# Moving GpSimd's two-tensor products to VectorE and ScalarE in a two-layer hybrid decoder step

## What is computed

```python
xn = rmsnorm(x, norm_mix)
zq, zk, zv, hq, hf, hi, hg, u, zg = split(xn @ w_in)
q, k = rope(rmsnorm(zq), pos), rope(rmsnorm(zk), pos)       # x1*cos - x2*sin, ...
p = e / (sum(e) + exp(sink - m))                            # attention weights
o_b = p @ v
qh = silu(hq)                                               # hq * sigmoid(hq)
S_new = exp(G_last) * S + (kc * exp(G_last - G)).T @ ic     # HGRN2 state; an output
o_a = rmsnorm(o, onorm) * silu(hg)
gates = sigmoid(zg)                                         # 3 x 1024 columns
x = x + sum_n(gates[n] * (branch[n] @ w_branch[n])) @ w_o
x = x + square(relu(rmsnorm(x) @ w_up)) @ w_down
```

## Time and profile before

| | |
|---|---|
| median of three runs | 1057.27 us (1057.12 to 1058.95) |
| the profiled execution: time, span | 1057.55 us, 1055.7 us |
| TensorE busy | 1010.8 us (96%), 7342 products |
| VectorE busy | 697.5 us (66%) |
| ScalarE busy | 501.2 us (47%) |
| GpSimd busy | 179.9 us (17%) |
| mean granted TensorE clock | 0.979 |

### The profile page before, as it was taken

The page is one execution under the profiler, slowest core; times in us unless marked ns, Lnnn a source line. Parts: engine busy times, 40 slices in busy tenths (PEclk is TensorE's granted clock), DMA queues, the critical chain, the costliest instruction groups (busy, mean ns, idle before and its releaser), DMA issues.

```text
span 1055.7 us, 18186 instructions
## 1 busy us (share of the span) xinstructions
PE 1010.8 (96%) x7342; PEld 976.8 (93%) x7342; DVE 697.5 (66%) x943; ACT 501.2 (47%) x740; POOL 179.9 (17%) x113
## 2 busy tenths in 40 slices
PE   6999998979999999999999999798899999999998
PEld 6989998969799999999998999798888999999998
DVE  6678776664887555555757787757558865555556
ACT  6428562236255444444554377332552554535354
POOL 0154021225430000000002441305055100000000
PEclk9999998989999999999999999999799999999999
DMA  7554542323365555555564553432334756555552
GB/s 274 178 185 137 183 150 80 101 80 92 121 249 174 164 161 170 162 165 160 170 216 132 175 202 102 132 107 73 100 100 127 271 161 176 162 161 161 173 162 84
DMA packets 43680, 161.87 MB, mean 153 GB/s; under 512 B 5120, under 2 KB 6400, under 8 KB 43040
## 3 DMA queue, kind: packets, MB, share of 16 engines
q1 hardware_dynamic: 42512, 151.73, 45.9%
q0 software_dynamic: 1104, 9.24, 2.2%
HBM read 152.69 MB, written 10.29 MB: 154 GB/s over the span
## 4 chain that ended last, share of the span: by engine, by line
PE 79%; DVE 12%; issue 4%; ACT 3%; POOL 1%; DMA 0%; DVEq 0%; ACTq 0%; POOLq 0%
PE pz L398 70%; PE pm L398 9%; DVE w_lo L949 3%; DVE arena L1149 2%; POOL arena L1438 1%; ACT w_hi L717 1%; DVE arena L1150 1%; DVE arena L1165 1%; DVE arena L1235 1%; PE pm L527 0%; DVE small L1124 0%; ACT a_hi L736 0%; DVE arena L1180 0%; ACT h_hi L926 0%; DVE arena L1199 0%
## 5 line engine op out<-in xcount | busy, mean ns | idle before, releaser
L398 PE MATMUL pz<-a_hi,w_hi 128*128 128x288 f32 x1376 | 418.3, 304 | 11.8 <-DVE w_lo L957 8.3
L949 DVE TENSOR_TENSOR w_lo<-raw,w_hi 128x1024 fp32r<-128x1024 f32 x267 | 351.4, 1318 | 92.8 <-ACT w_hi L717 92.5
L398 PE MATMUL pz<-a_lo,w_hi 128*128 128x288 f32 x1376 | 409.5, 298 | 0.0
L398 PE MATMUL pz<-a_hi,w_lo 128*128 128x288 f32 x1376 | 408.4, 297 | 0.0
L717 ACT ACTIVATE w_hi<-raw 128x1024 fp32r<-128x1024 f32 x267 | 279.5, 1051 | 193.4 <-PE pz L398 189.5
L398 PEld LDWEIGHTS pz<-a_hi,w_hi 128*128 128x128 f32 x1376 | 262.1, 190 | 15.6 <-issue 10.4
L398 PEld LDWEIGHTS pz<-a_lo,w_hi 128*128 128x128 f32 x1376 | 262.5, 191 | 1.2 <-issue 0.8
L398 PEld LDWEIGHTS pz<-a_hi,w_lo 128*128 128x128 f32 x1376 | 262.6, 191 | 0.0
L398 PE MATMUL pz<-h_hi,w_hi 128*128 128x288 f32 x768 | 230.0, 300 | 2.8 <-DVE h_lo L1244 2.8
L398 PE MATMUL pz<-h_lo,w_hi 128*128 128x288 f32 x768 | 227.2, 296 | 0.0
L398 PE MATMUL pz<-h_hi,w_lo 128*128 128x288 f32 x768 | 226.4, 295 | 0.0
(11 more groups left out here) (171 smaller groups left out, 728.9 us busy)
## 6 DMA issues: line engine op xcount, KB each, us to landing
raw<-in_w SPq DMA_DIRECT2D x268, 512.0 KB, 3.6
arena<-in_s SPq DMA_DIRECT2D x2, 2048.0 KB, 9.0
out_ss_out<-arena POOLq DMA_DIRECT2D x2, 2048.0 KB, 9.7
out_u_out<-arena POOLq DMA_DIRECT2D x2, 864.0 KB, 7.4
arena<-in_kcT SPq DMA_DIRECT2D x2, 512.0 KB, 6.0
arena<-in_vc SPq DMA_DIRECT2D x2, 512.0 KB, 7.4
out_kc_out<-in_kc_kept POOLq DMA_DIRECT2D x2, 496.0 KB, 10.2
out_vc_out<-in_vc_kept POOLq DMA_DIRECT2D x2, 496.0 KB, 11.1
```

The source lines that it names most:

```text
L398: return nc.tensor.matmul(out, a, b, start=start, stop=stop, **kw)
L949: tt(w_lo[:, r], raw[:, r], f(w_hi[:, r]), ALU.subtract).then_inc(s["w_lo"], 1)
```

## The change

GpSimd keeps the pooling sums, the memsets, the branch sums and its DMAs. All its other work on two tensors goes elsewhere: the cosine product, the normalising of the attention weights and the two products with sigmoids to VectorE; the masks `im` to ScalarE, as copies scaled by a column of `bmask`; the gate tiles are read by VectorE with the norm's factor, as all other tiles are, and `scale_gates` and `read_gate` are gone. The decay of the state is fused with the sum: VectorE does state x decay + new part for each sample and head (32 instructions per layer). TensorE's products for it and VectorE's updates stand in the first turn of the feed-forward, after units 1, 3, 5 and 7 and in turns 2 to 9; the masks are written in turns 54 to 61.

```diff
@@ tensor: unit, hgrn, ffn_turn
-                    elif U_GATE <= t4 < T_BR:
-                        pe.wait_ge(s["z_read_act"], read_act(l, t4))
                     else:
                         pe.wait_ge(s["z_read_dve"], read_dve(l, t4))
...
-                if 53 <= u <= 56:
-                    h = u - 53
-                    if h < 2:
-                        pe.wait_ge(s["o_rstd"], l + 1)
...
+            def sample_states(l, h):
+
+                if h < 2:
+                    pe.wait_ge(s["rstd"], 2 * l + 2)
+                    pe.wait_ge(s["o_rstd"], l + 1)
+                else:
+                    pe.wait_ge(s["snew_read"], 4 * l + (h - 1) + HEAD)
+                pe.wait_ge(s["imask"], 4 * l + (h + 1))
+                im = (KK, D1, X1, ZF)[h]
+                for half in range(2):
+                    last = mm(PM[2 * (h % 2) + half], ktok_s[0:NS, h], im[0:NS, half * 512:(half + 1) * 512])
+                last.then_inc(s["snew"], 1)
...
                     if first and j == 0:
-                        pe.wait_ge(s["snew_read"], 4 * l + 4 + HEAD)
                         norm_sum(2 * l + 2)
+                    if first and j in (1, 3, 5, 7):
+                        sample_states(l, j // 2)
@@ scalar
-                    act.wait_ge(s["gate_z"], 3 * l + (3 - n))
+                    act.wait_ge(s["z_read_dve"], read_dve(l, U_GATE + (3 - n) * KT - 1))
...
+                if 54 <= u < 62:
+                    h = (u - 54) // 2
+                    im = (KK, D1, X1, ZF)[h]
+                    for b in range(4 * (u % 2), 4 * (u % 2) + 4):
+                        last = act_fn(im[0:NS, b * P:(b + 1) * P], itok[0:NS, 2, h], ACT.Copy,
+                                      scale=c("bmask", slice(0, NS))[:, b:b + 1])
+                    if u % 2:
+                        last.then_inc(s["imask"], 1)
...
-                    if U_GATE <= u < U_BR:
-                        read_gate(l, u)
@@ vector
+                elif t >= U_GATE:
+                    out = gate_tile(t)
...
+                    tt(qk_rs.rearrange("p (j t) -> p j t", t=T), qk.rearrange("p (j t) -> p j t", t=T), bc(cos, 5),
+                       ALU.mult).then_inc(s["qk_cos"], 1)
...
+                for g in {18: (0, 1, 2, 3), 20: (4, 5, 6)}.get(u, ()):
+                    hs, o = (GRP, g * 4) if g < 2 else (2, 8 + 2 * (g - 2))
+                    v = p_samp if g == 6 else prob[:, g].rearrange("p (a n) -> p a n", a=hs)
+                    for a in range(hs):
+                        last = ts_(v[:, a], v[:, a], rec[:, o + a:o + a + 1], None, ALU.mult)
+                    last.then_inc(s["prob_n"], 1)
...
+                    tt(ZQ, ZQ, D0, ALU.mult).then_inc(s["hz_q"], 1)
...
+                if u == 30:
+                    dve.wait_ge(s["sig"], 3 * l + 3)
+                    tt(ZG, ZG, D1, ALU.mult).then_inc(s["silu_g"], 1)
...
-                    tt(S0v[:, :, h], S0v[:, :, h],
-                       pm[:, b0:b0 + 2].rearrange("p c (b n) -> p (c b) n", n=P), ALU.add).then_inc(s["snew_read"], 1)
+            def sample_states(l, j):
+
+                h, half = (j - 2) // 2, j % 2
+                if half == 0:
                     dve.wait_ge(s["snew"], 4 * l + (h + 1))
...
+                for b in range(4 * half, 4 * half + 4):
+                    z = PM[2 * (h % 2) + half][:, (b % 4) * P:(b % 4 + 1) * P]
+                    last = stt(S0v[:, b, h], S0v[:, b, h], es[:, b * H + h:b * H + h + 1], z, ALU.mult, ALU.add)
+                if half:
+                    last.then_inc(s["snew_read"], 1)
...
+                    if first and 2 <= j < 10:
+                        sample_states(l, j)
                     if j + LEAD < 16 or not last:
                         split(l, U_FFN + j + LEAD, i)
...
-                    if u < U_GATE:
+                    if u < U_BR:
                         read_tile(l, u)
...
-                with dve.Fori(0, FI - 1) as i:
-                    mlp(l, i, False, True)
+                mlp(l, 0, False, True)
+                with dve.Fori(0, FI - 2) as i:
+                    mlp(l, i + 1, False)
                 mlp(l, FI - 1, True)
```

More of the change, by code:

```diff
@@ L72 @@
 T_BR, T_O, T_FFN = 50, 74, 82
-ACT_READS = T_BR - U_GATE
-DVE_READS = U_GATE + (T_FFN - T_BR) + 16 * FI
+READS = T_FFN + 16 * FI
 C = {}
@@ L307, in read_dve @@
         def read_dve(l, t):
-            return l * DVE_READS + (t + 1 if t < U_GATE else t + 1 - (T_BR - U_GATE)) + HEAD
-        def read_act(l, t):
-            return l * ACT_READS + (t + 1 - U_GATE)
+            return l * READS + (t + 1) + HEAD
         def first_norm(j):
@@ L389, in _ @@
             for j0, j1 in pieces:
-                sp.wait_ge(s["z_read_dve"], DEPTH * DVE_READS + HEAD - (KT - j1))
+                sp.wait_ge(s["z_read_dve"], DEPTH * READS + HEAD - (KT - j1))
                 sp.dma_start(io["y"][:, j0:j1], x[:, j0:j1]).then_inc(s["y_out"], 16)
@@ L432, in unit @@
                     if t4 < 0:
-                        pe.wait_ge(s["z_read_dve"], l * DVE_READS + HEAD)
-                    elif U_GATE <= t4 < T_BR:
-                        pe.wait_ge(s["z_read_act"], read_act(l, t4))
+                        pe.wait_ge(s["z_read_dve"], l * READS + HEAD)
                     else:
@@ L745, in norm @@
                 act_fn(rstd[:], rstd[:], ACT.Exp, scale=-0.5).then_inc(s["rstd"], 1)
-            def read_gate(l, t):
-                act.wait_ge(s["unit_done"], l * UNITS + (t + 1) + HEAD)
-                act_fn(gate_tile(t), PZ[t % 4][:, 0:T], ACT.Copy).then_inc(s["z_read_act"], 1)
             def attention(l, u):
@@ L1051, in attention @@
                     nc.vector.reciprocal(rec, den).then_inc(s["rec"], 1)
+                    dve.wait_ge(s["rec"], l + 1)
+                for g in {18: (0, 1, 2, 3), 20: (4, 5, 6)}.get(u, ()):
[4 more added lines that the diff above has]
+                    last.then_inc(s["prob_n"], 1)
                 if u == 25:
@@ L1113, in hgrn @@
                 if u == 27:
+                    dve.wait_ge(s["sig"], 3 * l + 1)
+                    tt(ZQ, ZQ, D0, ALU.mult).then_inc(s["hz_q"], 1)
                     dve.wait_ge(s["sig"], 3 * l + 2)
@@ L1184, in hgrn @@
                     tt(a_lo[:, 0:4], hv(X0), f(a_hi[:, 0:4]), ALU.subtract).then_inc(s["oa_lo"], 1)
-                if 54 <= u <= 57:
-                    h = u - 54
+            def sample_states(l, j):
+                h, half = (j - 2) // 2, j % 2
+                if half == 0:
                     dve.wait_ge(s["snew"], 4 * l + (h + 1))
-                    dve.wait_ge(s["s0_decay"], l + 1)
-                    b0 = 2 * (h % 2)
-                    tt(S0v[:, :, h], S0v[:, :, h],
-                       pm[:, b0:b0 + 2].rearrange("p c (b n) -> p (c b) n", n=P), ALU.add).then_inc(s["snew_read"], 1)
+                for b in range(4 * half, 4 * half + 4):
[3 more added lines that the diff above has]
+                    last.then_inc(s["snew_read"], 1)
             def keep_diagonal(l):
@@ L1361, in _ @@
                 q5 = qk.rearrange("p (j t) -> p j t", t=T)
-                tt(qk_rs.rearrange("p (j t) -> p j t", t=T), q5, bc(cos, 5), ALU.mult).then_inc(s["qk_cos"], 1)
                 nc.gpsimd.memset(uext[:, :, 0:PAD], 0.0).then_inc(s["u_front"], 1)
@@ L1395, in _ @@
                 tt(pool_d[:, :, 0:PAD], first, uext[:, :, PAD:2 * PAD], ALU.subtract).then_inc(s["pool_first"], 2)
[L1397 to L1414, removed]
                 pool.wait_ge(s["sfin"], l + 1)
@@ L1421, in _ @@
                 pool.dma_start(io["sp_out"][l].rearrange("p h n -> p (h n)"), ZI[:, 0:512]).then_inc(s["sp_out"], 16)
[L1422 to L1431, removed]
                 for d in range(KT):
```

## The result

The changed kernel took 1025.09 us, the median of four runs (1025.03 to 1026.71), beside 1057.19 for the kernel before on the same chip: a ratio of 0.9685, with a 95% interval from 0.9667 to 0.9703. The forecast was 1027.0 with a range of 1014 to 1039. The profiled execution took 1025.03 us (span 1023.2), 32.5 under that of before; the mean granted clock rose from 0.979 to 0.995, GpSimd's busy time fell from 179.9 to 69.7 us, and VectorE's too, from 697.5 to 678.9, with more work on it.

What follows compares the result with a forecast made beforehand. TensorE was taken as the bound nearly everywhere, with stops caused by GpSimd holding VectorE. Removed 41.1 less 5.0, 3.5, 0.9 and 1.2 gives 30.5 us; 1057.5 - 30.5 = 1027 us, range 1014 to 1039.

Steps and rivals of the forecast that it cites:

- The cause: TensorE's stops at HGRN levels 0 and 5: GpSimd's products hold VectorE's instructions, though no wait names GpSimd.
- The removed 41.1 us: Both layers: split waits before unit 31 (2.6 us), four line 1166 waits (24.0) and slow clock behind them (14.5) go.
- Level 0, 2 x 2.5 us: HGRN level 0, each layer: VectorE's gate reading waits for unit 33's end, so TensorE waits 2.5 us; 5.0 given back.
- Its slow clock, 3.5 us as the half of 7.0: After level 0's wait, both layers: half the old slow-clock loss (4.0 + 3.0) stays, 3.5 us; ends 0 and 7.0.
- Levels 5 and 6 and the last keep, 0.9 us: Ahead of unit 48, one unit barely covers VectorE's chain: 0.15 us at each of three places, 0.9 us in all.
- The transposes, 1.2 us: Behind unit 20: normalising on VectorE delays the pooled branch's low halves, a new 0.6 us wait per layer, 1.2 us.
- The wait at the branches' end stays at 1.4: Branches' end, line 1244: TensorE's wait of 1.4 us stays as it is in the sum.
- Free by cover: Query, gate and cosine products, feed-forward state updates and ScalarE's masks fit in idle or covered time and cost nothing.
- level 0 comes free: Rival: level 0's wait falls under some 1.3 us, nothing slow follows: 1021 us; chance 0.18.
- The tied ring: Rival: VectorE's turn, ScalarE's split and the next turn form a ring stopping TensorE at all seven levels: 1079; chance 0.06.

Runs made afterwards that it cites:

- the small products: Cosine product, normalising of the probabilities and the two sigmoid products put back on GpSimd, against the changed kernel: 1034.23 us.
- the late reading: VectorE reads unit 33's gate tile behind that turn's state work and level 0 instead of ahead, against the changed kernel: 1017.78 us (0.9620).

## Why the prediction was right

**The cause** (GpSimd holds VectorE): right, and shown by putting the decay and the gate products back one at a time. The masks alone were not put back. The parts add up only roughly. By the medians they are +18.0 us for the decay and +9.1 for the small products (on different chips) and +6.4 for the gates (on one chip), 33.5 against 32.1 for all; by the profiled executions +17.8, +6.0 and +5.1, 28.9 against 32.5. Slow running that falls otherwise makes much of the difference: in the profiled execution of the small products level 0 of layer 1 has 0.3 us of it in place of 1.8, and the start of layer 2 none in place of 1.5.

**The removed 41.1 us**: right. All four stops on the level product of before went; level 0's became another, smaller one.

**Level 0, 2 x 2.5 us**: measured 2 x 2.2, at the place and by the mechanism named, as the late reading shows. **Its slow clock, 3.5 us as the half of 7.0**: 1.8 + 1.8 = 3.6. This was luck: with the same wait other executions had 0.3 or 3.4 us in layer 1 (the last section), and no row said a half.

**Levels 5 and 6 and the last keep, 0.9 us**: the list of waits has 0.5, all of it at the last keep (L1237), but the distance has 1.4. From level 5's products to the products of unit 50 it is 28.35 us (209.10 to 237.45), before 30.92 with 3.3 of slow running in it: 0.7 us a layer more. With the gate products back on GpSimd it is 27.62 again, so VectorE's gate readings cost it, as forecast; the size was too small.

**The transposes, 1.2 us**: the step that failed. Their first eight start at 95.86, before at 95.91, and take 1.09 in place of 0.87. From the units ahead (74.60, before 74.71) to the unit behind (96.96, before 96.78) it is 0.3 us more, in layer 2 as well: 0.6 in place of 1.2. VectorE's low halves did come 1.5 us later (95.30 against 93.75); the mistake was that two of four had to be done. In the program the first four transposes need one. The length of the normalising was forecast as 2.8 and came to 2.71, but for a wrong reason. By shape, on VectorE:

```profile
L1057 DVE TENSOR_SCALAR arena<-arena,small 128x256 f32<-128x256 f32 x16 | 4.5, 349 | 0.0
...
L1057 DVE TENSOR_SCALAR arena<-arena,small 128x128 f32<-128x128 f32 x16 | 3.3, 281 | 0.1
```

128 more columns cost 68 ns, 0.53 ns a column. The Trainium skill (VectorE: DVE Perf Modes, the perf-mode tier table) gives such products two a cycle, which at that page's 0.96 GHz is 0.52 ns: the trace agrees, and I had rejected it. The 358 ns for 288 columns of the earlier trace rows was one point, and by this rate some 205 ns of it are fixed time; a rate takes two.

**The wait at the branches' end stays at 1.4**: 1.57. But the slow stretch behind it in layer 1 went (28.38 us for 198 products before, 26.66 after), which the sum did not have: 1.7 us. It gave back 1.5 at the start of layer 2, where 24 products take 4.91 us in place of 3.39 behind a wait of VectorE's that was there before.

**Free by cover**: right for the updates, to 0.01 us. Four masks took 1.26 us and not 1.0; moving them away gained nothing. The sum had the move of the state into the feed-forward at nothing. Against standing in the mix with the same work on VectorE it brought 3.6 us; but before, VectorE had only four sums a layer there, so this is a cost avoided and no part of the 32.5.

In sum it is 32.5 us measured against 30.5. By the distances between the same points of the two chains, the changed kernel gained more than the forecast at the waits of levels 0 and 5 (0.9), at the transposes (0.6), and from the products of unit 50 to the start of layer 2 and to the end (2.1 and 0.6, of which 1.7 is the slow stretch that went). It gained less at levels 5 and 6 and the last keep (0.5), in the slow clock of level 0 (0.2) and at the starts of the layers (1.6, of which 1.5 is that of layer 2). Together this is 1.9 us.

The rival "level 0 comes free" gave 1021 us for a wait of about half the size and full clock; with no wait at all it is 1017.8. The tied ring (1079) did not come: levels 1 to 4 show no wait.

## What to carry to other kernels

Read GpSimd's timeline beside VectorE's: a VectorE instruction at several times its usual length that ends its own length after GpSimd's is held, and no list of waits names the holder. Where work moves to an engine whose program runs in order, ask what the first instruction of each turn waits for: a reading of 0.46 us in front of the turn cost 3.8 us a layer, since the chain behind it did not need that tile. And the loop through three engines that TensorE waited for was shortened by taking an engine out, not by clearing the road for it.

## What the hardware showed that I had not expected

A stop of 2.2 us at level 0 cost 0.3, 1.8 or 3.4 us of slow running in different executions, with the code up to there nearly the same. In the first profile of the changed kernel the 16 and 24 products behind it take 2.58 + 4.23 us. In its second profile, of the same code, they take

```profile
159.61 3.05 PE pm L393 x16
162.65 5.32 PE pz L393 x24
```

and in the run with the small products on GpSimd

```profile
164.54 2.00 PE pm L393 x16
166.54 3.25 PE pz L393 x24
```

The granted clock, by stretches of the trace (from:to, us, TensorE busy, its clock, DMA share, GB/s), shows it for a wait near 70 us that lasts equally long in both. The changed kernel:

```profile
60.00:80.00 20.00, 18.88 (x142) 1.00 0.50 167
```

and the run without updates, with identical code up to there:

```profile
60.00:80.00 20.00, 18.88 (x126) 0.91 0.52 173
```

So differences of 3 us between two kernels, and up to 6 here, are not to be read from a few executions, while the waits at level 0, at the last keep and at the branches' end repeat to 0.1 us in the runs that do not touch them. The waits of the first 80 us do not: one of them lasts from 1.2 to 2.2 us.

A near miss: GpSimd's write-out of the state and the two cache copies are now issued in the feed-forward, from 344.67 us on, and there ScalarE waited 6.9 us for weights, until 357.25. TensorE's list has no wait in that stretch; the split leads by three units. That the write-out held the weights up is argued from the times alone.
